# Expert output rows: from DRAM rows gathered at the end to 0/1 matrix products on chip, in one step of a streaming encoder layer

## What is computed

```python
g_idx = jnp.argmax(g_logits, axis=-1)                    # one of 4 groups
top_v, top_i = lax.top_k(e_sel, TOP_K_INNER)             # 2 of its 4 experts
top_w = jax.nn.softmax(top_v, axis=-1) * g_w
...
for e in range(N_EXPERTS):                               # 16 experts
    h = jax.nn.silu(xt @ w_gate[e]) * (xt @ w_up[e])     # 1024 -> 512
    y = y + combine[:, e:e + 1] * (h @ w_down[e])        # 512 -> 1024
...
x = layer_norm(ALPHA * x + y, ln2_g, ln2_b)
```

## Time and profile before

| | us |
|---|---|
| median of 3 timed runs | 622.02 (618.39, 622.02, 629.8) |
| the profiled execution, its time | 624.97 |
| its span, first to last instruction | 622.9 |
| PE busy in the span | 511.2 |
| DVE busy | 250.3 |
| ACT busy | 149.8 |
| POOL busy | 67.7 |
| HBM read / written, MB | 145.1 / 11.8 |
| mean granted clock of PE | 0.925 |

### The profile page before, as it was taken

One profiled execution on the slowest core, in us unless ns is written; L12 is line 12 of the kernel. 1 busy time (PEld: TensorE's weight loads), 2 busy tenths in 40 slices (PEclk: granted clock), 3 DMA queues, 4 the chain that ended last, 5 costly groups with the idle time before them and its releaser, 6 DMA issues.

```text
span 622.9 us, 9254 instructions
## 1 busy us (share of the span) xinstructions
PE 511.2 (82%) x3588; PEld 387.6 (62%) x3589; DVE 250.3 (40%) x529; ACT 149.8 (24%) x283; POOL 67.7 (11%) x87
## 2 busy tenths in 40 slices
PE   4789958999989896999952999989876699787860
PEld 1789944998989896988642655555443355453410
DVE  2926937688563444414354121111111121111187
ACT  3444339785624522100120010000000010000010
POOL 4151720000000000010004300000000000000300
PEclk9999979999999987999955999999979999999775
DMA  8327890233338747496194399999999999999622
GB/s 205 118 83 217 224 325 18 80 124 104 101 109 282 258 139 226 136 354 256 58 413 162 115 384 368 393 399 387 407 394 400 396 403 421 414 422 424 235 73 84
DMA packets 55212, 157.47 MB, mean 253 GB/s; under 512 B 3558, under 2 KB 36034, under 8 KB 51076
## 3 DMA queue, kind: packets, MB, share of 16 engines
q1 hardware_dynamic: 46464, 135.11, 58.3%
q0 software_dynamic: 4896, 13.92, 7.5%
q10 hardware_dynamic: 3812, 7.88, 3.5%
HBM read 145.10 MB, written 11.78 MB: 252 GB/s over the span
## 4 chain that ended last, share of the span: by engine, by line
PE 58%; DMA 24%; DVE 7%; ACT 4%; issue 4%; SPq 3%; DVEq 0%; POOLq 0%; ACTq 0%
PE bank L1041 18%; DMA expert_slots<-in_w_up 16%; PE bank L850 7%; PE bank L852 7%; PE bank L851 7%; PE bank L1004 7%; DMA expert_slots<-in_w_branch_rnn 3%; SPq L606 3%; DMA expert_slots<-in_w_in 2%; PE bank L1034 2%; DMA z_rows<-work 2%; PE bank L831 2%; PE bank L832 1%; PE bank L833 1%; DVE work L1443 1%
## 5 line engine op out<-in xcount | busy, mean ns | idle before, releaser
L1041 PE MATMUL bank<-expert_slots,work 128*64 128x256 f32 (+3 forms) x1584 | 189.5, 411 | 34.9 <-DMA expert_slots<-in_w_gate 11.6
L1041 PEld LDWEIGHTS bank<-expert_slots,work 128*64 128x64 f32 (+1 forms) x1584 | 106.8, 137 | 106.4 <-issue 47.8
L850 PE MATMUL bank<-z_high,weights_high 128*128 128x320 f32 (+1 forms) x320 | 101.4, 317 | 8.9 <-DVE weights_low L555 6.4
L852 PE MATMUL bank<-z_high,weights_low 128*128 128x320 f32 (+1 forms) x320 | 100.7, 315 | 0.0
L851 PE MATMUL bank<-z_low,weights_high 128*128 128x320 f32 (+1 forms) x256 | 79.5, 310 | 0.0
L555 DVE TENSOR_TENSOR weights_low<-expert_slots,weights_high 128x1024 fp32r<-128x1024 f32 (+1 forms) x54 | 60.2, 1140 | 40.2 <-ACT weights_high L549 39.9
L850 PEld LDWEIGHTS bank<-z_high,weights_high 128*128 128x128 f32 x320 | 61.7, 193 | 10.3 <-DVE weights_low L555 7.1
L1804 DVE SCALAR_TENSOR_TENSOR work<-work,bank 128x256 f32<-128x256 f32 (+1 forms) x18 | 7.3, 406 | 146.2 <-ACT work L1348 140.3
L549 ACT CAST weights_high<-expert_slots 128x1024 fp32r<-128x1024 f32 (+1 forms) x54 | 52.3, 987 | 52.7 <-DMA expert_slots<-in_w_in 18.0
L852 PEld LDWEIGHTS bank<-z_high,weights_low 128*128 128x128 f32 x320 | 61.4, 192 | 0.0
L851 PEld LDWEIGHTS bank<-z_low,weights_high 128*128 128x128 f32 x256 | 48.0, 188 | 0.0
(11 more groups left out here) (267 smaller groups left out, 578.5 us busy)
## 6 DMA issues: line engine op xcount, KB each, us to landing
expert_slots<-in_w_gate SPq DMA_DIRECT2D x16, 2048.0 KB, 28.0
expert_slots<-in_w_up SPq DMA_DIRECT2D x16, 2048.0 KB, 31.6
expert_slots<-in_w_down SPq DMA_DIRECT2D x15, 2048.0 KB, 26.6
expert_slots<-in_w_in SPq DMA_DIRECT2D x19, 1024.0 KB, 5.4
expert_slots<-in_w_branch_rnn SPq DMA_DIRECT2D x4, 1024.0 KB, 7.5
expert_slots<-in_w_out SPq DMA_DIRECT2D x4, 1024.0 KB, 5.2
expert_rows<-work ACTq DMA_DIRECT2D x30, 128.0 KB, 8.1
expert_rows<-work POOLq DMA_DIRECT2D x6, 384.0 KB, 9.1
```

The source lines that it names most:

```text
L850: nc.tensor.matmul(o, wh[:, k, :], xh, start=(k == 0), stop=False)
L852: mm = nc.tensor.matmul(o, wl[:, k, :], xh, start=False, stop=(k == kk - 1))
L1041: mm = nc.tensor.matmul(bank[m * j:m * j + m, cols], lhsT(k), rhs(k, j), start=(k == 0), stop=(k == kk - 1))
```

## The change

1. The DRAM buffer is gone, with its zero fills, the row DMAs, the 6 gathers, POOL's wait for them and the sums of L1863. An item's y stays on chip. ACT writes its rounded part (fp32r) and DVE the remainder into one 128-row operand `y_parts`: for each half of the columns, rounded rows lie in one 64 partitions and the remainder in the other (`high_part`, `low_part`). One fp32r product with a 0/1 matrix `own` (both 64-row halves hold the same code, so rounded part and remainder are summed in it) gives the rows of 128 tokens; PE does 3 token tiles x 2 column halves per item (`add_tile`), DVE adds each to the tokens with the weight (`add_sum`).
2. POOL builds `own` for each item from token places spread over all partitions (`own_of`: 4 tensor_scalar, 2 tensor_tensor of 128x320, 1 small copy). The spread itself is made once: DVE `diag`, two fp32 products with `ones`, two ACT copies; DVE also makes `w_table`.
3. A step on PE is `hidden(i)` with two tiles of `add(i-2)` in it, `turn(i+1)`, the load of the rest words, `down(i-1)`, `rest(i)`, `turn_hidden(i)`, the third tile of `add(i-2)`. The hidden rows have one PSUM bank instead of three.
4. `rest` is laid out like first rows: 32 products of 32x256 in two column tiles, 2 transposes, 8 products of 64x512, its own rounded part and remainder, and 6 products to add them, all before PE goes on.
5. At the end the adds of items 13 and 14 stand between the loop and item 15. ln2's two rows come as 4 KB rows after `y_high(14)` and are broadcast by 4 products of a row of ones (L1187 of the changed kernel) ahead of `hidden(15)`; ACT copies them.

The diff, cut to its core:

```diff
@@ POOL
-            for i in range(NE):
-                pool.dma_start(y_dram[CAP * i + FIRST:CAP * (i + 1), :], zeros).then_inc(zero_out, 16)
...
+            def own_of(i, s):
+                code = cst("lane")
+                for h in range(2):
+                    nc.gpsimd.tensor_scalar(same, slot_rows[:, 0, :], -float(CAP * i), code[:, h:h + 1], ALU.add, ALU.is_equal)\
+                        .then_inc(same_made, 1)
+                    nc.gpsimd.tensor_scalar(own[s][:, h, :], slot_rows[:, 1, :], -float(CAP * i), code[:, h:h + 1], ALU.add, ALU.is_equal)\
+                        .then_inc(same_made, 1)
+                    pool.wait_ge(same_made, 4 * own_of.n + 2 * h + 2)
+                    nc.gpsimd.tensor_tensor(own[s][:, h, :], own[s][:, h, :], same, ALU.add).then_inc(own_half, 1)
...
+            for i in range(1, NE):
+                if i + 2 < NE:
+                    pool.wait_ge(xt_full, i)
+                    gather(i + 2, (i + 2) % 3)
+                if i >= 3:
+                    pool.wait_ge(sum_free, 3 * (i - 2))
+                own_of(i, i % 3)
@@ PE
+            def add_tile(into, own_s, parts, j):
+                n = min(P, own_s.shape[-1] - P * j)
+                for h in range(2):
+                    mm = nc.tensor.matmul(into[h][0:n, :], own_s[:, P * j:P * j + n], parts[:, 512 * h:512 * h + 512], start=True, stop=True)
+                return mm
+            def add(i, s, j):
+                if j == 0:
+                    pe.wait_ge(low_y, i + 1)
+                    pe.wait_ge(own_made, i + 1)
+                wait_past(pe, sum_free, 3 * i + j)
+                add_tile(SUM, own_first(s), y_parts, j).then_inc(sum_full, 1)
...
+            def rest(i, s, n, b, summed, last=False):
+                for w, cols in ((w_gate, slice(0, 256)), (w_up, slice(256, 512))):
+                    for k in range(KD):
+                        for j in range(2):
+                            mm = nc.tensor.matmul(BB[FIRST * j:FIRST * j + REST, cols], xT[s][:, k, FIRST:CAP], w[s][:, k, 256 * j:256 * j + 256],
+                                                  start=(k == 0), stop=(k == KD - 1))
...
+                pe.wait_ge(low_yb, b + 1)
+                pe.wait_ge(own_made, i + 1)
+                wait_past(pe, sum_free, summed)
+                for j in range(3):
+                    if j == 1:
+                        pe.wait_ge(rest_sum_free, 3 * b + 1)
+                    add_tile(REST_SUM[j], own[s][:, 1, :], yr_parts, j).then_inc(rest_sum_full, 1)
+                pe.wait_ge(rest_sum_free, 3 * b + 3)
...
                 for s in range(3):
                     i = 3 * n + s
-                    hidden(i, s, n, ha_full)
+                    adds = not first or s == 2
+                    hidden(i, s, n, ha_full, (i - 2, (s + 1) % 3) if adds else None)
+                    turn(i + 1, (s + 1) % 3, n + (s + 1) // 3)
+                    words = rest_words(pe, i)
                     if not (first and s == 0):
                         down(i - 1, (s - 1) % 3, n if s else n - 1)
-                    turn(i + 1, (s + 1) % 3, n + (s + 1) // 3)
-                    maybe_rest(i, s, n)
+                    maybe_rest(i, s, n, 3 * (i - 2) + 2 if adds else 0, words)
                     turn_hidden(ha_made, i + 1, hta_full)
+                    if adds:
+                        add(i - 2, (s + 1) % 3, 2)
...
+            for j in range(3):
+                add(LAST - 2, (LAST - 2) % 3, j)
             down(LAST - 1, 2, NE // 3 - 1)
+            for j in range(3):
+                add(LAST - 1, (LAST - 1) % 3, j)
...
+            for i in range(2):
+                if i:
+                    pe.wait_ge(norm2_made, 2)
+                for h in range(2):
+                    nc.tensor.matmul(TB[h][:, :], ones[0:1, :], gb[0:1, i, 512 * h:512 * h + 512], start=True, stop=True)\
+                        .then_inc(norm2_full, 1)
@@ ACT
+            def high_part(parts, bank, made):
+                for h in range(2):
+                    half = slice(FIRST * h, FIRST * h + FIRST)
+                    nc.scalar.copy(parts[half, 512 * h:512 * h + 512], bank[half, :]).then_inc(made, 1)
@@ DVE
+            def low_part(parts, bank, high, n, made):
+                for h in range(2):
+                    half, other = slice(FIRST * h, FIRST * h + FIRST), slice(FIRST * (1 - h), FIRST * (1 - h) + FIRST)
+                    cols = slice(512 * h, 512 * h + 512)
+                    dve.wait_ge(high, 2 * n - 1 + h)
+                    inst = stt(parts[other, cols], bank[half, :], 1.0, parts[half, cols], ALU.mult, ALU.subtract)
+                inst.then_inc(made, 1)
+            def add_sum(into, full, count, s, j, done=None):
+                n = OUT_ROWS[j]
+                dve.wait_ge(full, count)
+                for h in range(2):
+                    half = rows[0:n, j, 512 * h:512 * h + 512]
+                    inst = stt(half, into[h][0:n, :], w_own[s][0:n, j:j + 1], half, ALU.mult, ALU.add)
```

More of the change, by code:

```diff
@@ L1363, in rest @@
+            def rest(b):
                 act.wait_ge(hb_full, b + 1)
-                run(th_b, BB[:, 0:P], ACT.Tanh, scale=0.5).then_inc(hb_tanh, 1)
+                for j in range(2):
+                    quarter = slice(FIRST * j, FIRST * j + REST)
+                    run(hid_b[quarter, :], BB[quarter, 0:256], ACT.Tanh, scale=0.5).then_inc(hb_tanh, 1)
                 act.wait_ge(yb_full, b + 1)
-                act.wait_ge(yb_out, 16 + 64 * b)
-                nc.scalar.copy(yo_b, BB[:, 0:256]).then_inc(yb_made, 1)
@@ L1831, in round_of @@
                     columns(i + 1, (s + 1) % 3)
-                    maybe_rest(i)
+                    if adds:
+                        add_first(i - 2, (s + 1) % 3, 1)
+                    maybe_rest(i, s)
                     hidden_columns(i + 1)
-            with dve.Fori(0, NE // 3) as n:
-                round_of(n)
+                    if adds:
+                        add_first(i - 2, (s + 1) % 3, 2)
+                    if not (first and s == 0):
+                        low_part(y_parts, YB, high_y, i, low_y)
```

337 lines of the change are left out of this document (167 added, 170 removed).

## The result

| | before | after |
|---|---|---|
| median of the timed runs, us | 621.68 | 669.94 (664.79 to 679.49) |
| ratio | | 1.076, 95% interval 1.072 to 1.080 |
| profiled execution / its span, us | 624.97 / 622.9 | 664.79 / 663.0 |
| PE / DVE / ACT / POOL busy, us | 511.2 / 250.3 / 149.8 / 67.7 | 559.9 / 339.9 / 164.0 / 168.4 |
| HBM read / written, MB | 145.1 / 11.8 | 141.44 / 2.87 |

The account below looks back on a forecast made before the run. Expert stage bound near both limits, by PE early and weight loads later, then an end of handshakes. Span 622.9 - 6.4 (front) + 20.7 (stage) + 16 (end) = 653.2, so 652 us predicted; own range 638 to 666, 8 in 10: 632 to 672.

Parts of the forecast that it names:

- Front, -6.4: Before the expert stage: without the zero fills a unit of projection weights lands earlier, -6.4 us, bounds 0 to 7.8.
- Routing, 0: Routing: DVE's diag and table, two fp32 products and two ACT copies lie beside item 0's gather, 0 us; uncovered 5.
- One step, 13.5: PE's step per item in the expert stage: with six adding products (1.4 us) 13.5 us, range 12.9 to 14.5.
- Bytes, -0.66 an item: Expert stage's DMA: an item's two row DMAs (256 KB) go, saving 0.66 us per item.
- The wait for L1798 goes, -0.98: In each PE step: turning ahead of `down` removes PE's wait for DVE's copy of the turned tokens, -0.98 us.
- The block, 21.2: Spare-rows block on PE, items 1 and 10: 21.2 us each instead of 7.4, bounds 17 and 25; first idles DMA.
- After the second block: Behind item 10's block: four steps of 13.5 us plus 1.6 for half clock; `turn_hidden(14)` ends 20.7 us later.
- The end, +16: From `turn_hidden(14)` to `hidden(15)`: a chain of adds, `down(14)` and broadcasts takes +27 us, before +11.0; so +16.
- the forecast's sum at full clock: The end's chain at 2.4 GHz: `hidden(15)` 22.8 us after `turn_hidden(14)`; 31 us at 1.2 GHz throughout.
- The queue covers the blocks: Rival, chance 0.12: loads hide the spare-rows blocks, the first ending by about 375 us; time about 623 us.
- Nothing new on the path: Rival, chance 0.07: blocks and end are covered, `hidden(15)` within 12 us of `turn_hidden(14)`; time 607 us.
- Cold: Rival, chance 0.12: waits inside the blocks and the end hold PE at 1.2 GHz; 652 + 17 = 669 us.

## Why the prediction was right, and what in it was wrong

- **Front, -6.4.** Right in size, -6.0 over the profiles, and in mechanism: the wait of 9.05 us is 1.08. ACT reaches its copies behind the wait at 83.45 instead of 90.36, and I had put 84.0. The first pair of profiles alone (327.2 and 339.5) would have said -12.2.
- **Routing, 0.** Right: PE's two products take 2.47 us at 323.00, and PE still waits 1.77 for the gather.
- **One step, 13.5.** 13.83. The mis-sized term is the adding product: a pair takes 0.66 us of PE (from 381.12 to 381.78), 0.33 a product, where I took 0.23 by columns from the 0.15 of the earlier trace rows. PE had a margin against the weights, so this counts only in the four steps behind the second block, 1.3 us.
- **Bytes, -0.66 an item.** Right by itself (9.9 us for 15 items): putting them back costs 10.3 us, 7.6 of them in the stage.
- **The wait for L1798 goes, -0.98.** Gone on PE, but the step "turning ahead of `down`" was priced on PE alone. With turning first the stream is 3% slower and the stage 6 to 8 us longer, which took back what the bytes gave. This is the step that failed. It is also the largest part of the stage's miss of 12 us (32.6 for 20.7): the bytes that I had let come in until item 10 are 4.6 (item 10's up products start 171.0 us after the first turning product, the forecast had 166.2), the two blocks 2.5, the steps 1.3 and the slow clock 1.4; 2.1 stay unassigned.
- **The block, 21.2.** 22.4 and 22.5. Products 7.10 (7.2), the first wait 2.26 (2.2), down 3.65 (3.4), parts 2.10 (2.0); the adds with their sums 6.3 where 5.3 were put. DMA ran dry as said, and PE's time counts, so the mechanism was right.
- **After the second block.** Four steps and 3.0 us of slow clock (587.75 - 529.47 less 4 x 13.83), where I added 1.6: the next gate products take 6.01 us for 3.67, at a granted clock of 0.74 from 520 to 540 us.
- **The end, +16.** +23.8. `hidden(15)` came 34.6 us after `turn_hidden(14)` was done (35.1 from its start), where I had +27, and above my other bound of +31. The chain had the parts I named. Missing was the gap at the branch (3.88). Too small was the clock's part: from 590 to 614 us it is 0.72, `down(14)` takes 5.07 (3.4), four of the six adds 1.0 to 1.2 (0.6), and the four broadcast products take 3.75 and 3.78 us a pair, the price of the same form at the start of the kernel (7.20 for four). Against the forecast's sum at full clock (+22.8) the gap is 3.9 us, the broadcast products 4.0, the adds about 2.5 and `down(14)` 1.7. The granted clock is 0.50 from 593.8 to 600 us, behind adds that waited 2.91 and 1.50, comes back during `down(14)`, and is 0.50 again from 608 to 626, over the last adds and the broadcast products (rows below this list). "Half of that at full clock" is shown by no row: the only other one of this form, at the start, has the same price while the trace gives a granted clock of 1.00 there, so how much of the 3.75 is the clock stays open. The rule of the Trainium skill quoted ahead of the rivals, from the page "TensorE: Matmul & The Clock Gate", section "Why this matters for your kernels", agrees with these rows in that the clock falls where PE keeps waiting; but here it was still at the full level up to 593.8, behind the longest wait (2.91), and fell behind a shorter one (1.50).
- **The rivals.** "The queue covers the blocks" failed because the block is 22 us and not 10; that blocks of 7.4 are covered is shown by the kernel before without them. "Nothing new on the path" needed `hidden(15)` within 12 us; it took 35. "Cold" came nearest in time (669), partly by luck. Its terms add up to 19 and not 17 (4 for each block, 2 for each of two steps, 4, 3), so 671. Of these the blocks gave 1.2 and 1.3 instead of 4 each, the steps behind them 0.9 and 3.0, the last products nothing (`down_last` 5.04 us for 6.7 before), and the end 7.6 instead of 4.

The clock at the end (columns as in the earlier trace rows):

```profile
596.00:600.00 4.00, 3.47 (x8) 1.28 (x10) 1.88 (x3) 0.00 (x0) 1.92 (x3) 0.50 0.01 2
600.00:608.00 8.00, 4.39 (x16) 1.25 (x12) 2.79 (x4) 1.16 (x2) 0.00 (x0) 0.93 0.01 2
608.00:626.00 18.00, 11.94 (x27) 4.67 (x28) 2.81 (x4) 2.34 (x4) 0.00 (x0) 0.50 0.01 2
```

## What to carry to other kernels

Work put into a step that runs level with the weight stream costs its PE time less the waits for weights that it takes over (here 30 us for 45), and releasing one load earlier didn't help where the next one waits for later work. A cheap row write hidden behind a stream costs its bytes (8 to 10 us here); a chain of handshakes at the end, with products between them that ran at the lower clock, cost more than twice that (24 us). Price a reordering on every queue that its releases feed, not only on the engine whose list is reordered, and don't believe a gain of 2% from one profile (613.0 us for 622.9 here, and no gain in 12 runs).

## What the hardware showed

- Busy share of the DMA engines is not throughput: at 1.02 they moved 402 GB/s in one order of the same work and 390 in another.
- At a branch over a long block that isn't entered PE stood for 3.88 us (0.18 without the block), in the kernel before 2.57 with item 15's matrix turned late. With the four broadcast products moved ahead of the branch it was 0.18 again; why is open.
- POOL's compare with a number per partition is dear, 1361 ns for 128x320 where I had about 870 from a row of 1024 elements; the matrix of an item takes 7.3 us of POOL in all. It stayed hidden:

```profile
L757 POOL TENSOR_SCALAR work<-work,const 128x320 f32<-128x320 f32 x32 | 43.5, 1361 | 126.7 <-DVE work L1878 125.0
```
